# Moving the second third of an adaLN product from TensorE to GpSimd, and loading the last four experts in 2 MB slots

## The reference

```python
mod = silu(c) @ w_ada + b_ada            # (1, 1024) @ (1024, 6144) -> sh1, sc1, g1, sh2, sc2, g2
h = rmsnorm(x, norm1_g) * (1 + sc1) + sh1                     # x: 256 tokens of 1024
proj = h @ w_in                          # (256, 1024) @ (1024, 6656): conv B, C, u, q, k, v, two gates
y_a = (cb * causal_dwconv(cc * cu)) @ w_out_conv
y_b = rmsnorm(diff_attention(q, k, v)) @ w_o_attn             # 8 heads, two softmaxes a head
x = x + g1 * ((sigmoid(ga) * y_a + sigmoid(gb) * y_b) @ w_merge)
h = rmsnorm(x, norm2_g) * (1 + sc2) + sh2
# top 4 of 32 experts: gate-up (1024 x 2048), clamped SwiGLU, down (1024 x 1024)
x = x + g2 * moe(h)
return rmsnorm(x, normf_g)
```

## Time and profile before

| | before |
|---|---|
| median of the runs | 1197.81 us |
| the profiled execution | 1198.26 us |
| its span, first to last instruction | 1196.5 us |
| TensorE busy | 1157.0 us (97%) |
| VectorE busy | 413.8 us (35%) |
| ScalarE busy | 208.8 us (17%) |
| GpSimd busy | 19.9 us (2%) |
| moved | 470.55 MB, 393 GB/s over the span |
| granted TensorE clock | 0.998 of full |

### The profile page before, as it was taken

The page is one execution under the profiler, slowest core; times in us unless marked ns, Lnnn a source line. Parts: engine busy times, 40 slices in busy tenths (PEclk is TensorE's granted clock), DMA queues, the critical chain, the costliest instruction groups (busy, mean ns, idle before and its releaser), DMA issues.

```text
span 1196.5 us, 15173 instructions
## 1 busy us (share of the span) xinstructions
PE 1157.0 (97%) x6133; PEld 524.9 (44%) x6133; DVE 413.8 (35%) x792; ACT 208.8 (17%) x331; POOL 19.9 (2%) x38
## 2 busy tenths in 40 slices
PE   7999999999999999999999999999999999999997
PEld 4787899984333333333333333333333333333332
DVE  4667776663232322222222222222222322222222
ACT  4346644341011010101010101010101101010001
POOL 1000010000000000000000000000000000000000
PEclk9999999999999999999999999999999999999999
DMA  9998457699999999999999999999999999999995
GB/s 337 393 374 326 170 188 245 245 393 368 428 422 431 428 432 427 437 426 434 431 428 433 426 437 427 426 427 428 429 436 425 436 428 432 432 427 435 422 426 234
DMA packets 53171, 470.55 MB, mean 393 GB/s; under 512 B 4479, under 2 KB 10060, under 8 KB 31894
## 3 DMA queue, kind: packets, MB, share of 16 engines
q1 hardware_dynamic: 50884, 467.99, 94.1%
q10 hardware_dynamic: 2258, 2.16, 0.6%
HBM read 469.08 MB, written 1.06 MB: 393 GB/s over the span
## 4 chain that ended last, share of the span: by engine, by line
PE 71%; DMA 24%; ACT 2%; SPq 1%; DVE 1%; issue 1%; DVEq 0%; ACTq 0%
PE ps L1104 25%; DMA expert<-in_w_down 17%; PE ps L1114 15%; PE ps L875 14%; DMA expert<-in_w_gate_up 6%; PE ps L1080 4%; PE ps L1052 3%; PE ps L1033 2%; PE ps L819 1%; PE ps L1060 1%; ACT r_cu L1358 1%; DMA ada_first<-in_w_ada 1%; PE ps L732 1%; SPq L489 1%; PE ps L1096 1%
## 5 line engine op out<-in xcount | busy, mean ns | idle before, releaser
L1104 PE MATMUL ps<-expert,r_work 128*64 128x512 f32 x2048 | 454.5, 595 | 5.5 <-DMA expert<-in_w_gate_up 4.6
L1104 PEld LDWEIGHTS ps<-expert,r_work 128*64 128x64 f32 x2048 | 141.3, 137 | 293.1 <-issue 283.2
L1114 PE MATMUL ps<-expert,r_work 128*64 128x512 f32 x1024 | 228.7, 596 | 10.2 <-DMA expert<-in_w_down 10.1
L1371 ACT ACTIVATE r_v<-r_v 128x512 f32<-128x512 f32 x32 | 20.1, 630 | 734.5 <-DVE r_v L1836 734.5
L1836 DVE TENSOR_SCALAR r_v<-ps 128x512 f32<-128x512 f32 x32 | 22.1, 692 | 326.7 <-PE ps L1104 326.7
L1114 PEld LDWEIGHTS ps<-expert,r_work 128*64 128x64 f32 x1024 | 70.0, 137 | 145.7 <-issue 123.7
L1503 DVE TENSOR_TENSOR w_lo<-stage,w_hi 128x2048 fp32r<-128x2048 f32 x36 | 82.2, 2289 | 38.3 <-ACT w_hi L1227 38.3
L875 PE MATMUL ps<-x_hi,w_hi 128*128 128x256 f32 x304 | 87.3, 287 | 1.0 <-issue 0.9
L875 PE MATMUL ps<-x_lo,w_hi 128*128 128x256 f32 x304 | 86.0, 283 | 0.0
L875 PE MATMUL ps<-x_hi,w_lo 128*128 128x256 f32 x304 | 85.9, 283 | 0.0
L1227 ACT ACTIVATE w_hi<-stage 128x2048 fp32r<-128x2048 f32 x36 | 68.9, 1913 | 92.9 <-PE ps L875 63.7
(11 more groups left out here) (230 smaller groups left out, 893.2 us busy)
## 6 DMA issues: line engine op xcount, KB each, us to landing
expert<-in_w_gate_up SPq DMA_DIRECT2D x44, 4096.0 KB
expert<-in_w_down SPq DMA_DIRECT2D x61, 2048.0 KB, 18.0
expert<-in_w_gate_up SPq DMA_DIRECT2D x40, 2048.0 KB, 38.0
stage<-in_w_in SPq DMA_DIRECT2D x24, 1024.0 KB, 7.0
stage<-in_w_ada SPq DMA_DIRECT2D x16, 1024.0 KB, 8.5
expert<-in_w_down SPq DMA_DIRECT2D x5, 1024.0 KB, 37.3
ada_first<-in_w_ada SPq DMA_DIRECT2D x16, 256.0 KB, 6.5
ada_first<-in_w_ada SPq DMA_DIRECT2D x8, 512.0 KB, 11.5
```

What stands on the lines that cost most here:

```text
L1104: mm = pe.matmul(ps[CAP * g:CAP * g + CAP, j, :], xg[:, 2 * (k % 4) + k // 4, :], buf[:, col:col + 512], start=False, stop=(k == KD - 1))
L1114: mm = pe.matmul(ps[CAP * half:CAP * half + CAP, bank, :], turned[:, ch, CAP * g:CAP * g + CAP], buf[:, col:col + 512], start=(q == 0), st ...
```

## The change

The second third of w_ada is no longer multiplied on TensorE. GpSimd multiplies each chunk by its values of silu(c) and adds it to an accumulator in `r_xn`; TensorE then sums the partitions with four products after chunk 18. Its chunks come two positions later in the stream and use buffers 3 and 4 alternately; panel chunks from 7 on use buffers 0 to 2. Since `r_xn` is now in use for longer, the early load of slot 2 moves from behind `w11` to behind `w20` and waits for that sum.

In the expert stage the block loads end one pair earlier, and the last four experts' gate-up weights are loaded and waited for slot by slot. In the last pair the gather and the transposes for the last expert are put between the up products of the one before it, and the transposes of the first one's activations between those of the last. Expert 30's last down piece is cut in two. The last of the four stores is issued by ScalarE's queue.

```diff
-LAST_PIECES = [((0, 4), (4, 6), (6, 8)), ((0, 2), (2, 4), (4, 6), (6, 7), (7, 8))]
+LAST_PIECES = [((0, 4), (4, 6), (6, 7), (7, 8)), ((0, 2), (2, 4), (4, 6), (6, 7), (7, 8))]
-ADA_AT = {7 + k: ("ada", 1, k) for k in range(KD)}
+ADA_AT = {9 + k: ("ada", 1, k) for k in range(KD)}
-ADA_SUMMED = 23
+ADA_SUMMED = {1: 18, 2: 23}
+FEW_FROM = 7
...
-    if STREAM[_n][0] == "ada" and not _wide:
+    if STREAM[_n][0] == "ada" and STREAM[_n][1] == 1:
+        _b = STAGE + STREAM[_n][2] % 2
+    elif STREAM[_n][0] == "ada" and not _wide:
         _b = WIDE - 1
+    elif STREAM[_n][0] == "w" and STREAM[_n][1] >= FEW_FROM:
+        _b = min(range(STAGE), key=lambda b: _last.get(b, -1))
...
-EARLY = {11: 2, 28: 0, 33: 1}
+EARLY = {20: 2, 28: 0, 33: 1}
...
-                eng.wait_ge(ada_used, KD * what[1] + what[2] + 1)
+                eng.wait_ge(ada_pool_added, what[2] + 1)
...
                 if early == 2:
-                    sp.wait_ge(x_turned, 1)
+                    sp.wait_ge(ada_used, KD + 1)
...
+            for p in range(2):
+                i = 2 * end_of_blocks + p
+                rest_of_next(i, p)
+                first_of_second(i, p, 0)
...
+            def ada_add(k):
+
+                wait_chunk(pool, ("ada", 1, k))
+                src = front_chunk(STREAM.index(("ada", 1, k)))[0][:, :]
+                if k == 0:
+                    pool.wait_ge(x_turned, 1)
+                    ins = nc.gpsimd.tensor_scalar(ada_acc[1], src, cs32[:, k, 0:1], None, ALU.mult)
+                else:
+                    own.done(nc.gpsimd.tensor_scalar(src, src, cs32[:, k, 0:1], None, ALU.mult))
+                    own.wait()
+                    pool.wait_ge(ada_pool_added, k)
+                    ins = nc.gpsimd.tensor_tensor(ada_acc[1], ada_acc[1], src, ALU.add)
+                ins.then_inc(ada_pool_added, 1)
+
+            pool.wait_ge(c_ready, 1)
             for h in range(H):
+                ada_add(h)
                 pool.wait_ge(osq_done, h + 1)
...
-                if n in ADA_AT and ADA_AT[n][1] == 1:
-                    ada_chunk(*ADA_AT[n][1:])
...
-            with pe.Fori(0, final) as m:
+            ahead_of_final = pe.value_load(last_pair[0:1, 1:2], min_val=E // 2 - 2, max_val=ROUNDS * E // 2 - 2)
+            with pe.Fori(0, ahead_of_final) as m:
                 pair(m)
-
-            up_product(2 * final, 0, final, True)
-            pe.wait_ge(st_ready, 2 * final + 1)
+            pair(ahead_of_final, 0)
...
+            up_product(2 * final, 0, final, 1, {4: [gather_last], 6: [turn_gathered_last]})
             pe.wait_ge(y_ready, 2 * final + 1)
             scatter(st[1], False)
-            next_tokens(2 * final + 1)
-            turn_act(2 * final, 3)
-            turn_gathered(2 * final + 1)
             gate_up_bias(2 * final + 1, 1)
-            up_product(2 * final + 1, 1, final, True)
+            up_product(2 * final + 1, 1, final, 1, {4: [turn_act_of_first]})
...
+            act.wait_ge(y1_out, 2)
+            act.dma_start(out_dram[1, :, 512:1024], x_sb[:, 1, 512:1024]).then_inc(stored, 16)
```

More of the change, by code:

```diff
@@ L256, in block_kernel @@
         csig = r_conv[:, 1552:1560]
-        ada_acc = r_gb[:, :]
+        ada_acc = {1: r_xn[:, :], 2: r_gb[:, :]}
         nfb = r_gb[:, 0:D]
@@ L452, in _, with load_slot @@
         def _(sp):
-            def load_slot(j, e, parity, last=False):
+            def load_slot(j, e, parity, apart=None):
                 n = slot(j, parity)
@@ L457, in load_slot @@
                     landed = down_landed[j - TWICE]
-                elif last:
-                    landed = last_landed[TWICE * parity + j]
+                elif apart is not None:
+                    landed = last_up(apart, parity, j)
                 else:
@@ L592, in blocks_of_second, with some_of_second @@
                     load_block(b, (i + 2) % E, parity)
-            def some_of_second(i, parity, first, end, last=False):
+            def some_of_second(i, parity, first, end, apart=None):
                 for j in range(first, end):
                     sp.wait_ge(up_used, UP_SLOTS * i + (j + 1))
-                    load_slot(j, (i + 2) % E, parity, last)
+                    load_slot(j, (i + 2) % E, parity, apart)
             for p in range(2):
@@ L643, in _ @@
                 sp.dma_start(out_dram[0, :, cols], x_sb[:, 0, cols]).then_inc(stored, 16)
[L644 to L647, removed]
+            sp.wait_ge(y1_out, 1)
+            sp.dma_start(out_dram[1, :, 0:512], x_sb[:, 1, 0:512]).then_inc(stored, 16)
             sp.wait_ge(stored, 16 * 2 * T)
@@ L723, in lam_column, with ada_sum @@
                 pe.matmul(ps[:, 7, 16:17], ones[0:1, :], lam_s[:, 4:5], start=True, stop=True).then_inc(lam_ready, 1)
[L725 to L730, removed]
-                for g in range(4):
[L732 to L741, removed]
+            def ada_sum(b):
+                pe.wait_ge(mod_ready, b + 2)
+                pe.wait_ge(ada_pool_added if b == 1 else ada_added, KD)
+                for g in range(4):
+                    m = pe.matmul(ps[32 * g:32 * g + 32, 6, :], ones[:, 0:32], ada_acc[b][:, 512 * g:512 * g + 512],
                                   start=True, stop=True)
@@ L1085, in _, with up_product @@
             final = pe.value_load(last_pair[0:1, 0:1], min_val=E // 2 - 1, max_val=ROUNDS * E // 2 - 1)
-            def up_product(i, p, m, last):
+            def up_product(i, p, m, apart, between={}):
                 pe.wait_ge(xg_ready, 2 * i + 1)
@@ L1097, in up_product @@
                         mm.then_inc(wp_turned, 1)
+                    for step in between.get(k, []):
+                        step()
                     if k % 2 == 0:
-                        wait_up(pe, k // 2, m, p, last)
+                        wait_up(pe, k // 2, m, p, apart)
                     buf = expert[slot(k // 2, p)]
@@ L1789, in _ @@
             own.wait()
-            own.done(v.tensor_scalar(over[:, 0:1], last_f, -1.0, None, ALU.add))
+            own.done(v.tensor_scalar(over[:, 0:2], iota[:, 0:2], last_f, -1.0, ALU.subtract, ALU.mult))
             own.wait()
             own.done(v.tensor_copy(last_pair[0:1, 0:1], last_f[0:1, :]))
-            own.done(v.tensor_copy(last_pair[0:1, 1:2], over[0:1, 0:1]))
+            own.done(v.tensor_copy(last_pair[0:1, 1:3], over[0:1, 0:2]))
             own.wait()
@@ L1839, in pair @@
                                     ALU.min, ALU.max).then_inc(gu_free, 1)
+                    if last and p == 0:
+                        v.wait_ge(gather_done, i + 2)
+                        tokens_in()
                     v.wait_ge(glu_ready, i + 1)
@@ L1847, in pair @@
                                     sig.rearrange("p (n c) -> p n c", c=4), ALU.mult).then_inc(act_ready, 1)
-                    if not (last and p == 1):
+                    if not last:
                         v.wait_ge(gather_done, i + 2)
@@ L1852, in pair @@
                     if last and p == 0:
+                        ready(m, 1, last)
                         continue
```

59 lines of the change are left out of this document (37 added, 22 removed).

## The result

The changed kernel takes 1264.7 us (median of four runs, 1263.51 to 1266.48) against 1198.27 us beside it: ratio 1.0557, 95% interval 1.0543 to 1.057. It is 66.4 us slower; 1227.8 was forecast. The profiled execution's span is 1261.7 us (before: 1196.5).

A forecast was written before the change was run, and what follows sets the result against it. The weight stream sets the pace and the front shifts it one for one. Terms +28.5 (VectorE held) - 3.0 + 1.5 + 1.1 + 4.7 - 2.8 = +30.0, so 1198.3 + 30.0 - 0.5 = 1227.8 us; range 1190 to 1234.

The forecast's parts named there:

- What bounds it: Whole kernel: weight loads set the pace, so a microsecond won or lost in the front shifts the end by one.
- What GpSimd's operations cost: Second third's sums on GpSimd: 1.8 us for a multiplication, 3.6 us for an addition over 128x2048.
- Who waits: Attention steps: VectorE stands for GpSimd's whole operations, 5.3 us a head, 31.8 for six, 28.5 after idle time.
- The first multiplication: Ahead of the attention stretch: three removed products count -3.0 us; no hold on VectorE was costed there.
- Behind the attention: SP's queue: slot 2's load waits for TensorE's sum, product 21 stands 4.7 us (bounds 0 and 7); sum 1.1 us.
- The late root: Last root of the attention: addition 7 delays it, 8.7 us root to root instead of 7.4, taken as +1.5 us.
- The experts: Last four experts: finer weight waits and interleaving gain 2.4 us, last store on ScalarE's queue 0.4, together -2.8 us.
- The clock: Whole kernel: the granted clock is full throughout and nothing in the change alters it.
- B: Front: no contention of weight, only the loop through the buffers; +5.1 before other terms, 1202.9 us; chance 0.14.
- A: Attention stretch: GpSimd yields and VectorE never stands; +15.9 there, +17.4 in all, 1215.2 us; chance 0.20.
- C: Attention stretch: add with multiplication under 4.5 us, VectorE not held, TensorE wins; 1192.8 down to 1188 us; chance 0.20.

The follow-up runs named there:

- x11: Changed kernel with transfers, buffers, waits and counts kept, but GpSimd's long sums replaced by tiny memsets, second third left out: 1201.82 us, ratio 1.003.
- x2: Changed kernel with GpSimd's seven in-place multiplications by the constant 0.5 instead of the silu(c) column: 1264.89 us, ratio 1.0556.
- x4: Changed kernel with the early load of slot 2 behind w22 instead of w20: 1256.16 us, ratio 1.0483.
- x3: Changed kernel with chunk 4 of the last third in stage buffer 3 instead of buffer 4: 1257.28 us, ratio 1.0492.
- x6: Changed kernel with each GpSimd multiplication and addition for chunks 1 to 7 replaced by a memset over 128x4096: 1247.36 us, ratio 1.0409.
- x7: Changed kernel with GpSimd's multiplications left out, chunks 1 to 7 added unscaled: 1234.19 us, ratio 1.0299.

## Why the prediction was wrong in size

**What bounds it: right.** A microsecond of the front is one of the end: 66.9 at the first up product, 65.2 at the span's end, and the windows of the expert stage unchanged.

**Where the forecast went off, by place.** Up to root 0 it said -3.0 us and the traces say +2.7; root 0 to root 6 +28.5 against +41.7; from root 6 to the first up product +7.3 (1.5 + 1.1 + 4.7) against +22.4; behind it -2.8 against -1.7. So 35 us are missing in the sum of +30.0, which had the direction and the main term right.

**What GpSimd's operations cost: the step that failed.** I took 1.8 us for a multiplication and 3.6 for an addition; they take 5.48 and 4.50. The 1.8 was what was left of the affine_select behind VectorE's operation, another operation and a subtraction of two ends, used as a price. By the step's own upper bound, the 3.11 us of that row, it would still have been short. The addition's 4497 ns, which I had set beside the sum from the Trainium skill (GPSIMD Engine Reference, 3.1), was the right one: the trace says 4.49 and 4.50 where nothing holds it. With the 9.06 us a head that the measured prices lead to, my sum comes to 1250.4 us, so the prices make some 23 of the 36.9 us by which the time was missed.

**Who waits: right, whole and in both directions.** 9.06 us a head instead of 5.3. For roots 0 to 6 my 28.5 was 41.7. With 9.06 a head my sum gives 6 x 9.06 - 3.3 = 51.1 us there; it over-counts, since the first two steps lasted only 11.6 and 12.6 us (102.83, 114.44, 127.06). The rule of the Trainium skill (SBUF — State Buffer, Who interferes with whom), that the second comer is blocked entirely, decided this case: the held scalings and combinations agree with it, one row of the last section doesn't.

**The first multiplication: missed.** The three products removed ahead of the stretch gave their 2.8 us (root 0 of x11 at 97.29 against 100.09). But the first multiplication, which itself took 7.04 us because it had begun under VectorE's subtraction (79.73 to 82.01; in x2, begun at its end, it took 5.49), held a two-column operation for 5.22, and root 0 came 2.7 later, not 3.0 earlier. I had costed the holds from step 9 on.

**Behind the attention: one wait found, one missed.** I followed SP's queue for slot 2 (4.7 us; x4 says up to 8.5, since it now meets a later sum), and the sum on TensorE cost the 1.1 (1.06). I didn't follow buffer 4: chunk 4 of the last third is the next user behind the last addition. The stretch lost 13.9 us, and x3 alone gave 7.4 back. Even with no sum late (x11) this stretch loses 11.1 us: the 6.3 of slot 2 and the sum on TensorE, where I had 4.7 + 1.1 = 5.8, and 4.6 for chunk 4, where I had nothing. So the removed products' 7.3 us could not pay for them. The late root was 11.3 us behind its neighbour (195.22 to 206.49) instead of 7.4: +3.9 for my 1.5.

**The experts: sign right, size -0.9 for -2.8**, and not beyond doubt. The wait of 2.2 us went, but TensorE found the next one, 1.8 us behind, as the prediction had it; what failed is the end, where 9.3 us of products follow a piece that lands at 1176.3.

**The clock: not foreseen.** I wrote that nothing here changes it. It was 0.79 of full in the window 105 to 195 of after, between its two levels of 1.2 and 2.4 GHz, with TensorE busy 49.4 of the 90 us, and 1.00 before, with TensorE busy throughout (89.15).

**The rivals.** B, the buffers without any holding, isn't what happened, because its condition failed. That its 1202.9 lies beside x11's 1201.82 is luck: B had sums of 5.4 us and steps of 9.6, x11 has no sums and steps of 8.26 and loses its time behind the attention. A (GpSimd yields) falls by VectorE's 5.49 and 4.87 us. C needed an add under 4.5 us with all it blocks; it costs 10 and blocks 9, and x11 shows that even a free one wouldn't have been faster with these queues. My range ended at 1234 because it allowed for no longer multiplication, the price with the weakest row, and for no wait at buffer 4.

## What to carry to other kernels

Before work moves to an idle engine, write down for each of its operations what it holds on its neighbour while it runs, and multiply by how often that neighbour's critical operations fall into it; here 10 us of GpSimd's work a head cost VectorE, which sets the pace, 9.06. Price each operation by a row of that same operation, and where there is none, let the range follow that one price. For each load that waits for a use, ask in which step it is issued and in which it is needed: one step of difference was 58 us here, over eight steps.

## What the runs showed of the hardware

VectorE's operations under a running one of GpSimd fall into three kinds. A tensor_scalar from SBUF to SBUF is held by a multiplication, an addition and a memset alike (5.49, 4.64 and 3.53 us above). An operation with two SBUF inputs is held by the addition (4.87), but not by the memsets (2.28, x6). Operations that read PSUM, and reductions, aren't held. In x7 the held operation is recorded 0.03 us ahead of the addition that holds it, so of starts this close the records don't tell which came first. From after, GpSimd's operations and then VectorE's:

```profile
104.08 5.45 POOL L701 TENSOR_SCALAR stage<-stage,r_cu 128x2048 f32<-128x2048 f32 x1
...
121.15 4.62 POOL L704 TENSOR_TENSOR r_xn<-r_xn,stage 128x2048 f32<-128x2048 f32 x1
...
127.06 0.92 POOL L671 TENSOR_SCALAR small<-small 128x2 f32<-128x2 f32 x1 [1.28 <-ACT r_work L1311]
```

```profile
105.34 0.68 DVE L1553 TENSOR_TENSOR r_work<-ps,r_bias 128x512 f32<-128x512 f32 x1
106.06 0.42 DVE L1556 TENSOR_REDUCE small<-r_work 128x2 f32<-128x256 f32 x1
...
106.99 2.95 DVE L1541 TENSOR_TENSOR w_lo<-stage,w_hi 128x2048 fp32r<-128x2048 f32 x1
...
123.99 3.93 DVE L1541 TENSOR_TENSOR w_lo<-stage,w_hi 128x2048 fp32r<-128x2048 f32 x1 [5.74 <-ACT w_hi L1259]
```

Under the multiplication the PSUM addition (0.68) and the reduction (0.42) keep their times. The subtraction that began during the addition ended 2.15 us after it (127.92 against 125.77), nearly its whole 2.28: it had been standing. And the root's 0.19 us became 0.92, up to the end of that subtraction. For operations with two SBUF inputs the multiplication is the odd case. A subtraction that began under it at 106.99 took 2.95 us, more than the 2.28 of a free one, but it ended at 109.94; held up to the multiplication's end (109.53) it would have ended near 111.8. By the rule of the Trainium skill (SBUF — State Buffer, Who interferes with whom) it should have been held, since the multiplication reads SBUF too. It was only delayed, and why stays open.
